# Last down projection: the block sums of the weights move from GpSimd to VectorE, and pairs of weight blocks get places of their own

## The reference, cut to what matters

```python
def _conv_ffn(x, w_up, conv_w, conv_b, w_down):
    hproj = _causal_dwconv(x @ w_up, conv_w) + conv_b
    gate, val = hproj[..., :D_FF], hproj[..., D_FF:]
    return (jax.nn.silu(gate) * val) @ w_down          # (1024 x 2816) @ (2816 x 1024)
...
        x = _layernorm(DN_ALPHA * x + ffn, ln2_g[layer], ln2_b[layer])
```

## Time and profile before

| | us |
|---|---|
| median of 3 runs | 2902.18 (2901.0 to 2903.54) |
| the profiled execution | 2901.78 |
| its span | 2900.0 |
| PE busy | 2797.4 (96%) |
| DVE busy | 2061.4 (71%) |
| POOL busy | 411.0 (14%) |

### The profile page before, as it was taken

The page is one execution under the profiler, slowest core; times in us unless marked ns, Lnnn a source line. Parts: engine busy times, 40 slices in busy tenths (PEclk is TensorE's granted clock), DMA queues, the critical chain, the costliest instruction groups (busy, mean ns, idle before and its releaser), DMA issues. The chain is left out here.

```text
span 2900.0 us, 45821 instructions
## 1 busy us (share of the span) xinstructions
PE 2797.4 (96%) x17767; PEld 2364.1 (82%) x17767; DVE 2061.4 (71%) x3174; ACT 1262.7 (44%) x2266; POOL 411.0 (14%) x297
## 2 busy tenths in 40 slices
PE   9999988999999999999999999999999999999798
PEld 7888878888888888888878877899988888888686
DVE  6544455665799999636589965455548999997978
ACT  5333255743454444332456643455433544444232
POOL 0000084230000000000000010455401000000521
PEclk9999999999999999999999999999999999999999
DMA  4333262524312222444423432522042122125542
GB/s 177 116 116 117 73 217 58 153 92 141 139 66 88 78 83 80 185 159 149 145 81 117 153 117 82 172 90 92 15 155 108 66 88 87 74 87 196 207 171 87
DMA packets 156454, 339.01 MB, mean 117 GB/s; under 512 B 35744, under 2 KB 69728, under 8 KB 145632
## 3 DMA queue, kind: packets, MB, share of 16 engines
q1 hardware_dynamic: 137680, 321.54, 31.5%
q10 hardware_dynamic: 18576, 14.75, 1.7%
HBM read 252.17 MB, written 84.05 MB: 116 GB/s over the span
## 5 line engine op out<-in xcount | busy, mean ns | idle before, releaser
L845 DVE TENSOR_TENSOR even_in_w_lo<-even_in_raw_left,even_in_w_hi 128x512 fp32r<-128x512 f32 x80 | 49.9, 687 | 88.2 <-ACT even_in_w_hi L770 88.2
L1792 POOL TENSOR_TENSOR ffn_down_rstd<-ffn_down_rstd,ffn_down_power 128x1 f32<-128x1 f32 x7 | 7.5, 1067 | 662.2 <-DVE ffn_down_rstd L1727 662.2
L1625 PE MATMUL ffn_down_acc<-two_hi,ffn_a_hi 128*128 128x512 f32 x320 | 98.7, 390 | 1.9 <-DVEq L1692 1.2
L728 PE MATMUL even_in_acc<-even_in_w_hi,even_x_hi 128*128 128x512 f32 x256 | 99.6, 389 | 0.0
L729 PE MATMUL even_in_acc<-even_in_w_lo,even_x_hi 128*128 128x512 f32 x256 | 99.6, 389 | 0.0
L730 PE MATMUL even_in_acc<-even_in_w_hi,even_x_lo 128*128 128x512 f32 x256 | 99.6, 389 | 0.0
L1625 PE MATMUL ffn_down_acc<-two_lo,ffn_a_hi 128*128 128x512 f32 x320 | 98.6, 389 | 0.0
L1625 PE MATMUL ffn_down_acc<-two_hi,ffn_a_lo 128*128 128x512 f32 x320 | 98.5, 389 | 0.0
L1698 DVE TENSOR_TENSOR ffn_a_lo<-ffn_a_raw,ffn_a_hi 128x512 fp32r<-128x512 f32 x38 | 26.3, 692 | 101.3 <-ACT ffn_a_hi L1576 101.3
L3653 DVE SCALAR_TENSOR_TENSOR even_mixed<-even_mixed,odd_qkv_taps 128x1023 f32<-128x1023 f32 (+2 forms) x72 | 92.1, 1281 | 4.9 <-ACT even_mixed L3487 3.2
L1576 ACT CAST ffn_a_hi<-ffn_a_raw 128x512 fp32r<-128x512 f32 x38 | 23.7, 623 | 145.0 <-PE ffn_down_acc L1625 137.9
(11 more groups left out here) (782 smaller groups left out, 9277.4 us busy)
## 6 DMA issues: line engine op xcount, KB each, us to landing
ffn_w_raw<-in_ffn_up SPq DMA_DIRECT2D x42, 1024.0 KB, 4.8
ffn_down_w_raw<-in_ffn_down SPq DMA_DIRECT2D x40, 512.0 KB, 3.5
odd_mixed<-in_ffn_down SPq DMA_DIRECT2D x30, 512.0 KB, 4.4
hp<-even_in_stage SPq DMA_DIRECT2D x13, 1024.0 KB, 4.2
even_out_w_raw<-in_ev_w_out SPq DMA_DIRECT2D x22, 512.0 KB, 3.5
hidden<-even_mixed SPq DMA_DIRECT2D x22, 512.0 KB, 2.6
ffn_w_raw<-in_od_w_qkv SPq DMA_DIRECT2D x11, 1024.0 KB, 5.7
hidden<-odd_mixed SPq DMA_DIRECT2D x22, 512.0 KB, 2.6
```

What stands on the lines that cost most here:

```text
L728: pe.matmul(to, hi[:, tok], wh, start=(opens and k == 0), stop=False, skip_group_check=not opens)
L845: dve.tensor_tensor(w_lo[:, p % 2, k], source(i)[:, k], f32(w_hi[:, p % 2, k]), ALU.subtract).then_inc(lo_ready, 1)
L1625: mm = pe.matmul(acc[:, t, n], aa[:, s, tok], ww[:, s, n * NB:(n + 1) * NB], start=(opening and aa is a_hi and ww is w_hi), stop=(last and ...
```

## The change

- The ring is replaced by a table of places: `place(q)`. There are ten, the eight lent tiles and two more of the stage's own (`w_own`). Pairs 0 to 4 of P7's weights each have two places to themselves: pair 0 the lent tiles 6 and 7, pair 1 the two own ones, pairs 2 to 4 the tiles 0 to 5. Pair 5 comes after pair 0 in tiles 6 and 7. Blocks 12 and on go round the own two and tiles 0 to 3.
- SyncE issues pairs 0 and 1 and their left weights ahead of `lead.run`, and each later pair right behind its rows: rows 2, pair 2, rows 3, pair 3, four residual tiles, the wait, rows 4, pair 4, rows 5, pair 5. The loads of gain and bias wait until the last split of P7 (step 11) is done, since pair 5 lies in their place.
- VectorE makes all weight sums, with the same three kinds of instructions. GpSimd keeps the eight small powers of the layer norm.
- In VectorE's loop the splits of step c come first, and the sums for step c + 2 behind them.

```diff
@@ project_blocks
-        w_ring = lent[:, 0:RING].rearrange("p e (k n) -> p e k n", n=HALF)
+        w_lent = lent.rearrange("p e (k n) -> p e k n", n=HALF)
+        w_own = sc.sbuf("w_own", [P, 2, 2, HALF])
...
+        def place(q):
+            if q < PAIRS:
+                return (6, 8, 0, 2, 4, 6)[q // 2] + q % 2
+            return (8, 9, 0, 1, 2, 3)[(q - PAIRS) % 6]
+        def last_in(q):
+            return [e for e in range(q) if place(e) == place(q)]
         def ring(q, j):
-            return w_ring[:, q % RING, 0:size(j)]
+            e = place(q)
+            return (w_lent[:, e] if e < TT else w_own[:, e - TT])[:, 0:size(j)]
@@ sync, load_ring
+                if last_in(q):
+                    before = last_in(q)[-1]
+                    if before < PAIRS:
+                        sp.wait_ge(w_sum, before + 1)
+                        if before % 2:
+                            sp.wait_ge(w_lo_done, BLOCKS * P7 + before // 2 + 1)
+                    else:
+                        sp.wait_ge(w_lo_done, BLOCKS * P4 + before - PAIRS + 1)
@@ sync, the order of loads
             for j in range(2):
                 load_a_kept(j)
                 load_a(0, j)
-            lead.run("sync", sp)
-            for j in range(2):
                 load_ring(2 * j)
                 load_ring(2 * j + 1)
                 load_w_kept(j)
-            for j in range(2, BLOCKS):
+            lead.run("sync", sp)
+            for j in range(2, 4):
                 load_a(0, j)
+                load_ring(2 * j)
+                load_ring(2 * j + 1)
...
-            for q in range(4, 2 * BLOCKS):
-                load_ring(q)
+            for j in range(4, BLOCKS):
+                load_a(0, j)
+                load_ring(2 * j)
+                load_ring(2 * j + 1)
...
+            sp.wait_ge(w_lo_done, BLOCKS * (P7 + 1))
             sp.dma_start(gain_b, gain.broadcast_to([P, D])).then_inc(affine_in, 16)
@@ vector (sum_w likewise, from GpSimd)
+            def first_sums_w(j):
+                wait_ring(dve, 2 * j)
+                wait_ring(dve, 2 * j + 1)
+                dve.tensor_tensor(ring(2 * j + 1, j), ring(2 * j, j), ring(2 * j + 1, j), ALU.subtract).then_inc(w_sum, 1)
+                dve.wait_ge(w_sum, 2 * j + 1)
+                dve.wait_ge(w_kept_in[j], 16)
+                dve.wait_ge(w_lo_done, BLOCKS * P1 + j + 1)
+                dve.tensor_tensor(kept(w_kept, j), kept(w_kept, j), ring(2 * j + 1, j), ALU.add).then_inc(w_sum, 1)
...
+                split_lo(c)
                 if after in (P7, P6, P5):
                     sum_a(after, j)
-                split_lo(c)
+                if after == P7:
+                    first_sums_w(j)
+                if after in (P4, P5):
+                    sum_w(after, j)
```

More of the change, by code:

```diff
@@ L1819, in project_blocks @@
     ENDING = 3
-    RING = 6
+    PAIRS = 2 * BLOCKS
     P1, P7, P6, P4, P5, P2, P3 = range(ORDER)
@@ L1833, in project_blocks @@
         acc = sc.psum("acc", [P, 2, HALF_T, NB])
-        w_ring = lent[:, 0:RING].rearrange("p e (k n) -> p e k n", n=HALF)
+        w_lent = lent.rearrange("p e (k n) -> p e k n", n=HALF)
+        w_own = sc.sbuf("w_own", [P, 2, 2, HALF])
         gain_b, bias_b = lent[:, 6], lent[:, 7]
         a_kept_in, w_kept_in, a_in = ([sc.sem(f"{part}_in{j}") for j in range(BLOCKS)] for part in ("a_kept", "w_kept", "a"))
-        w_in = [sc.sem(f"w_in{e}") for e in range(RING)]
+        w_in = [sc.sem(f"w_in{e}") for e in range(TT + 2)]
         left_in, whole_in, right_in = sc.sem("left_in"), sc.sem("whole_in"), sc.sem("right_in")
@@ L1895, in wait_ring @@
         def wait_ring(eng, q):
-            eng.wait_ge(w_in[q % RING], 16 * (q // RING + 1))
+            eng.wait_ge(w_in[place(q)], 16 * (len(last_in(q)) + 1))
         code = ctx.enter_context(nc.Block())
@@ L1930, in load_ring @@
                 k = 2 * j + down
-                sp.dma_start(ring(q, j), w[:, k:k + size(j), cols]).then_inc(w_in[q % RING], 16)
+                sp.dma_start(ring(q, j), w[:, k:k + size(j), cols]).then_inc(w_in[place(q)], 16)
             for s in range(2):
@@ L1957, in _ @@
                 load_a(1, j)
-                load_ring(2 * BLOCKS + j)
+                load_ring(PAIRS + j)
+            sp.wait_ge(w_lo_done, BLOCKS * (P7 + 1))
             sp.dma_start(gain_b, gain.broadcast_to([P, D])).then_inc(affine_in, 16)
@@ L2067, in sum_a, with sum_w @@
                     dve.tensor_tensor(of, held, of, ALU.subtract).then_inc(a_sum, 1)
+            def first_sums_w(j):
[6 more added lines that the diff above has]
+                dve.tensor_tensor(kept(w_kept, j), kept(w_kept, j), ring(2 * j + 1, j), ALU.add).then_inc(w_sum, 1)
+            def sum_w(i, j):
+                q = BLOCKS * (2 if i == P4 else 3) + j
+                wait_ring(dve, q)
+                dve.wait_ge(w_sum, 2 * j + 2)
+                dve.tensor_tensor(ring(q, j), ring(q, j), kept(w_kept, j), ALU.subtract).then_inc(w_sum, 1)
             def split_lo(c):
@@ L2154, in _ @@
         def _(pool):
[L2155 to L2170, removed]
             pool.wait_ge(power_set, 1)
```

## The result

The changed kernel takes 2882.91 us (median of 4 runs, 2878.66 to 2885.14) against 2902.86 for the kernel before, run beside it (4 runs, 2901.0 to 2905.2). The ratio is 0.9928, interval 0.9914 to 0.9942: **20 us faster**, where 21.1 were forecast. The profiled execution took 2882.41 us with a span of 2880.6. Two further groups of runs on other occasions gave 0.9931 (0.9918 to 0.9943) and 0.9928 (0.9915 to 0.9941).

A forecast was written before the change was run, and what follows sets the result against it. TensorE loses 22.1 us in P7 and early P6 to late VectorE splits and slow clock; less 1.0 us of waits left, 21.1 us off 2902.2 gives 2881.1 us, range 2879.5 to 2888.

The forecast's parts named there:

- The loss of 22.1 us in one stretch: P7 and start of P6: 147 matmuls take 55.4 us where 33.3 would do, through six waits and slow clock.
- The waits left in P7: Steps 7 to 9 on TensorE: 0.2 + 0.4 + 0.4, about 1.0 us, each too short to cost clock.
- VectorE's stretch is GpSimd's: VectorE's 128x1024 subtractions take 3.4 us against 1.22 because GpSimd reads SBUF beside them; moving the sums ends it.
- The three causes: VectorE late in P7: stretched beside GpSimd, row sum queued ahead of splits, ScalarE and SyncE held to GpSimd's pace.
- Ten places: Loads of P7: pairs 0 to 4 load without waiting for a sum; SyncE took 23.34 us for eight blocks.
- "Its end gives nothing" (later products): P4 and P5, steps 16 to 27: GpSimd's interference was hidden in VectorE's two-step lead, so ending it gains nothing.
- the waits of steps 11 and 12: Start of P6: VectorE needs 3.4 us a step against 5.44, so steps are ready early and these waits go.
- Rival 2: Transfers were the bound anyway; only VectorE's order helps, 6 us, time 2896; chance 0.07.
- The rate of loads: Loads in P7: 391 GB/s from the trace, 1.34 us per 512 KB, against the skill's about 358 GB/s.
- The store that moved behind six loads: Store of hidden, some 8 us later: 2.4 us of queue time, cost taken as 0, 1.3 if a load slips.
- the chances of its ways to be faster: Forecast with rival 4 0.66, rival 1 0.22, rival 2 0.07; faster in all given as 0.94.
- the 2.7 and 1.8 us named for slower loads: Step 7 at about 358 GB/s: wait of 2.7 us, 1.8 us of clock lost, sum then 17.8.

The follow-up runs named there:

- e4: The changed kernel run again unaltered as reference; 0.9931 of the kernel before.
- e12: The changed kernel run a third time unaltered as reference; 0.9928 of the kernel before.
- e6: The changed kernel with VectorE's weight splits of steps 4 to 9 done twice; 0.9944 of the kernel before.
- e8: The changed kernel with P7's sums made one step ahead of use in place of two; 0.9923 of the kernel before, 2882.11 us.
- e2: The changed kernel with all weight sums back on GpSimd, gain's load waiting for them; 0.9977 of the kernel before.
- e10: The changed kernel with six unused 128x1024 subtractions on GpSimd, after pair 1's sums; 0.9967 of the kernel before.
- e7: The changed kernel with all sums ahead of the step's splits on VectorE; 0.9951 of the kernel before.
- e3: The changed kernel with the old ring of six places and the old order of loads; 0.9956 of the kernel before.
- e5: The changed kernel with its ten places but the old order of loads; 0.9950 of the kernel before.
- e1: The kernel before with only VectorE's splits moved ahead of the row sum; 0.9994 of the kernel before.
- e9: The changed kernel with the twelve weight sums of P4 and P5 back on GpSimd; 0.9972 of the kernel before.

## Why the prediction was right, and where it was not

- **The loss of 22.1 us in one stretch.** Right: the stage is 21.0 us shorter (20.9 and 21.1 in e4 and e12), and the sum said 21.1. That it agrees to 0.1 is partly luck. In the first profile P7 and P6 gave 21.8 us and the opening took 0.8 back, where the sum had the opening unchanged. The time's own interval, 17 to 25 us, is wide beside that: the start of the stage shifts by some us from one execution to the next, so the 20 of the medians and the 21 of the stage can't be told apart.
- **The waits left in P7.** Forecast 1.0 us over steps 7 to 9; measured 0.7, 1.7 and 0.8. The working by the order of loads held within 0.2 us for pair 2, and within 1.3 for step 6, where more waits for single loads came in than I had put down. The opening and P7 together lose 3.3, 3.4 and 3.3 us in these profiles, where I had 2.7: a slow opening of TensorE gives VectorE a lead that it uses up in P7, so the small waits there depend on the opening. e6 and e8 show that this chain is what is left: longer by one instruction a step it costs some 3 us more, freed from the next pair's load it costs nothing.
- **VectorE's stretch is GpSimd's.** Shown by e2 and e10. The Trainium skill, "SBUF — State Buffer", section "Who interferes with whom", calls the port pair that VectorE and GpSimd share an exclusive lock. The rows agree in so far as the two engines go in lockstep, one instruction each per 2.8 or 3.3 us, and the two times nearly add (1.2 and 2.4 us alone, 3.3 beside each other).
- **The three causes.** They don't add. GpSimd out of the way, the order of VectorE is worth 6 to 7 us (e7) and the order of loads 6 to 8 (e3, e5); with GpSimd in, the row sum's part of the first is worth nothing (e1), and all of the change but the sums' move 4 to 9 (e2). Most of the gain needed GpSimd's sums gone.
- **Ten places.** I said they let pairs load without waiting for a sum, and took that for part of the cure of SyncE's 23.34 us. e5 against e3 shows that with sums at VectorE's pace and the old order of loads the wait for a place doesn't bound; the order of issue does.
- **"Its end gives nothing" (later products).** This step failed, though the sum did not feel it. I had put P4's sums with steps 16 to 21, where VectorE would do them, and not looked at when GpSimd did them. In the kernel before five of them ran right behind P6's, from 2714 to 2730, under steps 9 to 11:

```profile
2714.32 15.61 POOL L2158 TENSOR_TENSOR odd_mixed<-odd_mixed,ffn_down_w_kept 128x1024 f32<-128x1024 f32 x5
```

  e9 prices P4's and P5's sums at 11 to 13 us in the changed kernel, all of it under P4's: with them on GpSimd 8 of the 20 us are left. I had counted the waits of steps 11 and 12 as going, but for the sake of P7's and P6's sums. What they cost in the kernel before, beside the others, was not run by itself. Over half of the gain hangs on sums that I had called free.
- **Rival 2** had its price wrong: the order alone gives 0 and not 6 us.
- **The rate of loads** is 390 GB/s again in the window of P7, as I took from the trace. The store that moved behind six loads cost no more than the 2.4 us of queue time that I gave it, since pair 2 behind it landed within 0.2 us of the working.
- **Two small sums** of the prediction don't come out, and neither enters the forecast: the chances of its ways to be faster add up to 0.95, not 0.94, and 22.1 less the 2.7 and 1.8 us named for slower loads is 17.6, not 17.8.

## What to carry to other kernels

Move work to a second engine only with a look at what it does to the first one while it runs: an instruction on GpSimd with SBUF inputs cost the one beside it on VectorE 1.7 to 2.2 us, more than the 1.14 that VectorE needs for the same sum. An engine that runs ahead as soon as its data lands may do its work at the worst time, as P4's sums did here; look in the trace at when it runs, not at who wants the result. And a wait that is taken away while a slower chain runs beside it in its own time can come back whole, as in e1, so test the edits together as well as alone.

## What the runs showed of the hardware that I had not expected

How TensorE's granted clock answers to a wait is not settled by the wait's length. Waits of 0.69, 1.33 and 1.34 us (e6) and 1.42 (e1) were followed by matmuls at full speed (2.4 GHz). Those of 2.37, 2.60 and 5.80 (e1), 2.65 and 3.48 (e3), 5.02 (e7) and 8.46 (e10) were followed by some 3 us at half of it (1.2 GHz; the granted clock is 0.50 from 2702.1 to 2705.3 in e1). But the waits of 3.21 us in e1 and 3.12 us in e9 were not, and neither were the idle times of 2.26, 2.46 and 3.00 us ahead of the stage's first matmul in e3, e2 and e1, while 1.84 and 1.94 us were in e4 and e8. At the opening of the stage the loss ran from 0.1 to 2.9 us; by what rule the runs don't show.
